# A hybrid attention / Fourier / product-key step on one core: two of five block rankings are moved in among the output projections

## The reference

```
h   = rmsnorm(x, norm1_g) * (1 + sc1) + sh1
q, k, v, f = split(h @ w_in)
x  += g1 * (concat(headnorm(diff_attention(q, k, v)), fourier_mix(f)) @ w_out)     # "merge"
h2  = rmsnorm(x, norm2_g) * (1 + sc2) + sh2
q   = (h2 @ w_query)                      # 8 heads x 2 halves x 128
s   = q . sub_keys                        # 128 scores for each head and half
s1, i1 = top16(s[:, :, 0]);  s2, i2 = top16(s[:, :, 1])
top_s, pos = top16(s1[i] + s2[j])         # 16 of the 16 x 16 pairs
idx = i1 * 128 + i2 (at pos);  g = softmax(top_s)
a   = gelu(expert_u[idx] . h2);   x += g2 * sum(g * a * expert_v[idx])
y   = rmsnorm(x, final_g)
```

## Time and profile before

| | us |
|---|---|
| time, median of 3 runs | 1900.49 (1897.9 to 1902.98) |
| time of the profiled execution | 1900.14 |
| its span | 1898.2 |
| busy in the span: TensorE, VectorE, ScalarE, GpSimd | 1740.1, 1522.8, 681.9, 794.9 |
| merge starts on TensorE | 360.28 |
| first ranking done, dense gates start | 503.91 |
| last dense gates stored, issued | 745.43 |
| first dense sum | 806.77 |

### The profile page before, as it was taken

The page is one execution under the profiler, slowest core; times in us unless marked ns, Lnnn a source line. Parts: engine busy times, 40 slices in busy tenths (PEclk is TensorE's granted clock), DMA queues, the critical chain, the costliest instruction groups (busy, mean ns, idle before and its releaser), DMA issues.

```text
span 1898.2 us, 29868 instructions
## 1 busy us (share of the span) xinstructions
PE 1740.1 (92%) x9942; PEld 1490.9 (79%) x9942; DVE 1522.8 (80%) x3093; ACT 681.9 (36%) x1135; POOL 794.9 (42%) x646
## 2 busy tenths in 40 slices
PE   4789998897899999389999999999999999999994
PEld 2477746547788888279999999999999999999993
DVE  0342127334999999879999999999999999999997
ACT  1132226301367674223333333333333333333332
POOL 1300000000000000267887887778666666666661
PEclk9989989899999999689999999999999999999997
DMA  9921200520044445699999999999999999999993
GB/s 358 386 80 50 89 0 1 214 85 23 1 90 90 90 109 130 226 353 408 405 402 392 405 400 405 407 403 403 394 407 407 407 402 398 403 399 407 405 403 138
DMA packets 253538, 520.89 MB, mean 274 GB/s; under 512 B 113953, under 2 KB 130977, under 8 KB 252193
## 3 DMA queue, kind: packets, MB, share of 16 engines
q1 hardware_dynamic: 178016, 249.00, 36.9%
q0 software_dynamic: 73728, 268.47, 35.7%
q10 hardware_dynamic: 1730, 2.59, 0.4%
HBM read 488.54 MB, written 31.46 MB: 274 GB/s over the span
## 4 chain that ended last, share of the span: by engine, by line
PE 52%; DVE 25%; issue 13%; DMA 6%; ACT 3%; DVEq 1%; SPq 0%; POOL 0%; ACTq 0%; POOLq 0%
DVE arena L1155 12%; PE ps L1522 9%; PE ps L1521 9%; PE ps L1520 9%; PE ps L1440 5%; PE ps L1421 4%; DMA arena_w<-in_w_mod 4%; PE ps L1491 3%; DMA U_in<-in_expert_uT 2%; PE ps L1275 2%; PE ps L1279 2%; PE ps L1276 2%; PE ps L1319 1%; DVE V_lo L1117 1%; DVE C_lo L1130 1%
## 5 line engine op out<-in xcount | busy, mean ns | idle before, releaser
L1520 PE MATMUL ps<-hT_hi,U_hi 128*128 128x384 f32 x1024 | 344.4, 336 | 29.5 <-DVE U_lo L1112 29.5
L1522 PE MATMUL ps<-hT_hi,U_lo 128*128 128x384 f32 x1024 | 344.5, 336 | 0.0
L1521 PE MATMUL ps<-hT_lo,U_hi 128*128 128x384 f32 x1024 | 343.7, 336 | 0.0
L1520 PE MATMUL ps<-V_hi,C_hi 128*128 128x512 f32 x768 | 300.4, 391 | 11.0 <-DVE C_lo L1130 11.0
L1522 PE MATMUL ps<-V_hi,C_lo 128*128 128x512 f32 x768 | 302.3, 394 | 0.0
L1521 PE MATMUL ps<-V_lo,C_hi 128*128 128x512 f32 x768 | 302.3, 394 | 0.0
L1520 PEld LDWEIGHTS ps<-hT_hi,U_hi 128*128 128x128 f32 x1024 | 193.0, 188 | 34.6 <-issue 29.7
L732 ACT CAST V_hi<-V_in 128x1024 fp32r<-128x1024 f32 x128 | 135.1, 1055 | 235.9 <-PE ps L1522 235.9
L458 POOL DMA_INDIRECT arena<-in_expert_u,idxn x128 | 171.5, 1340 | 99.1 <-DVE arena L1144 37.8
L740 ACT ACTIVATE act_t<-ps 128x384 f32<-128x384 f32 x128 | 63.0, 492 | 410.0 <-PE ps L1522 410.0
L458 POOL DMA_INDIRECT arena<-in_expert_v,idxn x128 | 159.5, 1246 | 93.1 <-DVE arena L1155 41.1
(11 more groups left out here) (230 smaller groups left out, 3233.2 us busy)
## 6 DMA issues: line engine op xcount, KB each, us to landing
U_in<-in_expert_uT SPq DMA_DIRECT2D x128, 512.0 KB, 9.1
V_in<-in_expert_v SPq DMA_DIRECT2D x128, 512.0 KB, 6.4
arena_w<-in_w_mod SPq DMA_DIRECT2D x12, 2048.0 KB, 12.4
gates_scratch<-arena_w SPq DMA_DIRECT2D x6, 4096.0 KB, 20.8
gate_in<-gates_scratch SPq DMA_DIRECT2D x128, 192.0 KB, 7.4
arena_w<-in_w_in SPq DMA_DIRECT2D x4, 2048.0 KB, 12.4
arena_w<-in_w_query SPq DMA_DIRECT2D x1, 7168.0 KB, 20.6
arena_w<-in_w_out SPq DMA_DIRECT2D x2, 2048.0 KB, 7.8
```

The source lines that it names most:

```text
L1520: nc.tensor.matmul(out, hi, rhi, start=start, stop=False)
L1521: nc.tensor.matmul(out, hi, rlo, start=False, stop=False)
L1522: return nc.tensor.matmul(out, lo, rhi, start=False, stop=stop)
```

## The change

The order of the rankings becomes 0, 1, 2, 3, 4. Rankings of block 0 and 1 stand among the merges: TensorE's list is now written out by hand, halves of merges between query groups, with turns of h2 where a block's h2 is first needed. Dense gates of blocks 1, 2, 3 stand beside the rankings of 2, 3, 4, and no ranking stands alone behind them. The fetched blocks stay 0 and 4, in the other order.

To allow that: merges use PSUM banks 4 to 7; x is loaded into H2 itself, so h2 of a block overwrites x1 in place and waits until x1 of that block is stored (`s_spill[b]`); squares are taken by halves. In the last ranking all 32 quads stand in the first three groups; hT_lo and two U_lo stand between the third and the fourth. The sum over one-hot rows (`tensor_reduce`) becomes four additions. SyncE's list issues U of groups 2 and 3, all of XF and fing ahead of H2s, V and gates.

```diff
-SPARSE = (4, 0)
+SPARSE = (0, 4)
-ORDER = (1, 2, 3, 4, 0)
-FIN = (4, 0, 1, 2, 3)
+ORDER = (0, 1, 2, 3, 4)
+FIN = (0, 4, 1, 2, 3)
+def dense_at(n):
+    return n - 1 if 2 <= n <= NDEN + 1 else 0
@@ sync
-            sp.wait_ge(s_wT, len(UNITS))
+            sp.wait_ge(s_chunk_used, DFT_C + 1)
             for b in range(NBLK):
-                sp.dma_start(X[:, b], xall[b * P:(b + 1) * P, :]).then_inc(s_xr[b], 16)
+                sp.dma_start(H2[b], xall[b * P:(b + 1) * P, :]).then_inc(s_xr[b], 16)
...
-                sp.dma_start(x1_d[b * P:(b + 1) * P, :], X[:, b]).then_inc(s_spill, 16)
+                sp.dma_start(x1_d[b * P:(b + 1) * P, :], H2[b]).then_inc(s_spill[b], 16)
...
             for b in range(1, NDEN + 1):
+                if b == NDEN:
+                    sp.wait_ge(s_fill2, B2.total)
+                    for j in range(2):
+                        load_u(j, j)
@@ vector: make_h2
+                link(dve.tensor_tensor(ss[:, b:b + 1], ss2[:, 0, b:b + 1], ss2[:, 1, b:b + 1], ALU.add))
                 dve.wait_ge(s_rstd2, b + 1)
-                link(dve.scalar_tensor_tensor(out=H2[b], in0=X[:, b], scalar=rstd[:, b:b + 1],
+                dve.wait_ge(s_spill[b], 16)
+                link(dve.scalar_tensor_tensor(out=H2[b], in0=H2[b], scalar=rstd[:, b:b + 1],
@@ vector: select
-                    link(dve.tensor_reduce(sel[:, w, :], onehot, AX.X, ALU.add))
+                    for n_ in (8, 4, 2):
+                        link(dve.tensor_tensor(onehot[:, :, 0:n_], onehot[:, :, 0:n_], onehot[:, :, n_:2 * n_], ALU.add))
+                    link(dve.tensor_tensor(sel[:, w, :], onehot[:, :, 0], onehot[:, :, 1], ALU.add))
@@ vector: the new order
+            merged(0, 0)
+            merged(0, 1)
+            make_h2(0)
...
+            merged(1, 0)
+            merged(1, 1)
+            make_h2(1)
+            ranked(0, 0)
+            merged(2, 0)
+            ranked(0, 1)
+            merged(2, 1)
+            ranked(0, 2)
+            make_h2(2)
+            merged(3, 0)
+            ranked(0, 3)
+            merged(3, 1)
+            dve.wait_ge(s_step, steps[0])
+            select(0)
+            make_h2(3)
+            gate_weights(0)
+            ranked(1, 0)
+            merged(4, 0)
+            ranked(1, 1)
+            merged(4, 1)
+            ranked(1, 2)
+            make_h2(4)
+            ranked(1, 3)
@@ vector: the last ranking
+                    for g in range(3):
+                        key_tops(n, g, bd, (2, 3, 2) if g else (0, 2, 2))
+                        dve.wait_ge(s_step, steps[0])
+                        pair_tops(g, bd, (1, 2, 1) if g else (2, 2, 2))
+                    dve.wait_ge(s_hThi, 1)
...
+                    split_u(0, 0)
+                    ranked(n, 3)
+                    split_u(1, 1)
+                    dve.wait_ge(s_step, steps[0])
+                    select(n, 0)
@@ tensor: the new order
+            merge(0, 0)
+            merge(0, 1)
+            merge(1, 0)
+            turn(0)
+            merge(1, 1)
...
+            turned(0)
+            part(0, 0)
+            score(0, 0)
+            merge(2, 0)
+            part(0, 1)
+            merge(2, 1)
+            score(0, 1)
+            turn(1)
+            part(0, 2)
+            merge(3, 0)
+            score(0, 2)
+            part(0, 3)
+            merge(3, 1)
+            score(0, 3)
+            turned(1)
+            part(1, 0)
+            merge(4, 0)
+            score(1, 0)
+            part(1, 1)
+            merge(4, 1)
+            score(1, 1)
+            part(1, 2)
+            score(1, 2)
+            turn(2)
+            part(1, 3)
+            score(1, 3)
+            turn(3)
+            turn(4)
+            turned(2)
+            part(2, 0)
+            score(2, 0)
+            part(2, 1)
+            score(2, 1)
+            pe.wait_ge(s_gated, 2 * NBLK)
```

More of the change, by code:

```diff
@@ L210, in program @@
         H2s = cutout(XO + 2 * D, D)
[L211 removed]
+        h2row = (H2[0], H2s)
         XF = cutout(MO, 5120).rearrange("p (b d) -> p b d", b=NBLK)
@@ L382, in _ @@
                 load_u(n, n % 2)
+            for b in range(NBLK):
+                sp.dma_start(XF[:, b], x1_d[b * P:(b + 1) * P, :]).then_inc(s_xf, 16)
+            sp.dma_start(fing, final_g.unsqueeze(0).broadcast_to([P, D])).then_inc(s_fing, 16)
+            sp.wait_ge(s_acc0, 1)
+            sp.wait_ge(s_h2out, 16)
+            sp.dma_start(H2s, h2_d).then_inc(s_h2in, 16)
+            for n in range(2, 4):
                 sp.wait_ge(s_vlo, n - 1)
                 load_v(n, n % 2)
[L385 to L391, removed]
+            sp.wait_ge(s_c, 1)
+            load_gates(2, 0)
             with sp.Fori(2, PAIRS) as i:
@@ L693, in sel_out, with softmax_exp @@
                     one_hot((b - 1) * QUADS + p)
[L695 to L702, removed]
+            def softmax_exp(n):
+                act.wait_ge(s_top, n + 1)
+                act.activation(top[:, :, :], top[:, :, :], ACT.Exp).then_inc(s_gexp, 1)
+            squares2(0)
+            turned(0)
+            squares2(1)
+            query_out(0, 0)
+            query_out(0, 1)
+            turned(1)
+            squares2(2)
+            query_out(0, 2)
+            query_out(0, 3)
+            squares2(3)
+            query_out(1, 0)
+            softmax_exp(0)
+            query_out(1, 1)
+            query_out(1, 2)
+            squares2(4)
+            turned(2)
+            query_out(1, 3)
+            turned(3)
+            turned(4)
+            query_out(2, 0)
+            query_out(2, 1)
+            softmax_exp(1)
+            for n in range(2, NBLK):
+                bd = dense_at(n)
+                sel_out(bd)
+                ahead = [(n, 2), (n, 3)] + ([(n + 1, 0), (n + 1, 1)] if n + 1 < NBLK else [])
                 for p in range(QUADS):
@@ L1097, in _ @@
             dve.memset(onesb[0:1, :], 1.0)
[L1098 to L1106, removed]
+            merged(1, 0)
[22 more added lines that the diff above has]
+            dve.wait_ge(s_step, steps[0])
+            select(1)
+            gate_weights(1)
             def split_u(n, r):
@@ L1416, in _, with merge, turn @@
             chunk_ready(OUT_C + 1)
[L1417 to L1421, removed]
-                                                start=(k == 0), stop=(k == KD - 1))
-                    last.then_inc(s_fill2, 1)
-            for b in range(NBLK):
+            def merge(b, half):
+                i = 2 * b + half
+                out = ps[:, 4 + i % 4, :]
+                if i >= 4:
+                    pe.wait_ge(s_gated, i - 3)
+                for k in range(KD):
+                    last = nc.tensor.matmul(out, mixT[:, k, b * P:(b + 1) * P], chunk[:, (OUT_C + half) % WRING, k, :],
+                                            start=(k == 0), stop=(k == KD - 1))
+                last.then_inc(s_merge, 1)
+            def turn(b):
                 pe.wait_ge(s_h2, b + 1)
@@ L1495, in dense_gates, with turned, part @@
                     differences(b, p + LR - 1)
+            def turned(b):
+                pe.wait_ge(s_act2, B2.emptied(B2.pos[("h2T", b, 1)])[1])
+            def part(b, g):
+                for j in range(4):
+                    query(b, g, j)
+            merge(0, 0)
[3 more added lines that the diff above has]
+            merge(1, 1)
             pe.wait_ge(s_wq, 16)
```

127 lines of the change are left out of this document (69 added, 58 removed).

## The result

The changed kernel takes 1908.36 us (median of 5 runs, 1905.19 to 1909.59) where the kernel before takes 1897.9 beside it (5 runs, 1897.44 to 1902.98): a ratio of 1.0046, 95% interval 1.0035 to 1.0057. It is slower, by 9 us when taken by the ratio and by 10.5 when taken by the medians. The forecast was 1909.5; rival A is what happened.

A forecast was written before the change was run, and what follows sets the result against it. TensorE was taken to bound the kernel. First dense sum at 825.1 instead of 806.8, less 8.9 regained by gelu of group 5, gave +9.4 on 1900.14: 1909.5 us, own range 1905 to 1914, overall range 1894 to 1917.

The forecast's parts named there:

- rival A: Whole kernel: the forecast itself, 1909.5 us, own range 1905 to 1914; chance 0.42.
- What bounds the kernel: Dense stages: TensorE with its queries sets the time, 80.4 us a stage, with VectorE close behind.
- The start: +37: Up to the first dense gates: TensorE's work, waits of 7.5 and 8, restarts of 4; gates at 540.9, 37 later.
- The additions: Rankings on VectorE: additions take 1.5 against 2.29 for the reduce, 1.6 off each ranking; full stages stay 80.4.
- The last stage: 70.9: Third dense stage: two query groups, then ScalarE sets the pace at 1.65 a quad; 70.9 against 80.4 before.
- H2s lands 27.2 behind the store: Queues behind the last store: 10.3 MB at about 410 GB/s, 25.2, plus 2 of latency; H2s lands at 820.8.
- What comes back: 8.9: First dense sum to gelu of group 5: U of group 4 no longer late, 34.9 instead of 43.8, 8.9 regained.
- The sum: +9.4: Whole kernel: first dense sum at 825.1 less 806.8, less 8.9 regained, gives +9.4 on 1900.14.
- B: Behind the last store: H2s or later loads come earlier by other queue sharing or overtaking, 1897 to 1903; chance 0.24.
- C: At the start: TensorE runs without its two waits and restarts, 19.5 earlier, 1890; one wait, 1900; chance 0.13 for faster.
- D: Start or last stage: VectorE is late at more scores or falls behind, 5 to 10 more, 1915 to 1920; chance 0.16.
- E: Dense stages: they hang on VectorE and the additions pay, 3 to 5 less than forecast, 1905; chance 0.05.

The follow-up runs named there:

- e9: The changed kernel with the four additions over one-hot rows put back to a tensor_reduce: 1909.26 us, ratio 1.0051 to the kernel before.
- e3: The changed kernel with the turn of block 0 behind the fourth merge half instead of the third: 1900.72 us, ratio 1.0011.
- e5: e3 with the turn of block 4 behind a query group of block 2, and score (2,1) moved into the dense stage: 1898.1 us, ratio 0.9996.
- e4: The changed kernel with the copy hT_hi of the last stage made by VectorE instead of ScalarE: 1906.57 us, ratio 1.0044.
- e1: The changed kernel with VectorE waiting for H2s only at its first use, in the second quarter of the fetched rows: 1900.78 us, ratio 1.0009.
- e6: The kernel before with only the changed kernel's SyncE list behind the last store of gates: 1897.54 us, ratio 0.9991.
- e7: e1 with the five XF and fing loaded one at a time, nine pairs apart, in the expert loop: 1893.48 us, ratio 0.9974.
- e8: The changed kernel with the edits of e5 and e7 in one: 1885.95 us, ratio 0.9934 to the kernel before.
- e2: e1 with XF and fing loaded in one piece four pairs before the expert loop's end: 1903.97 us, ratio 1.0022.

## Why the prediction was right, step by step

- **What bounds the kernel.** TensorE does; held, with a small rest. The two full stages took 699.00 - 540.04 = 159.0, that is 79.5 each, against a forecast of 80.4 from the earlier trace rows. The step said that the additions don't touch them; by e9's trace they take 0.8 off the two together. The other 1.0 is not accounted for.
- **The start: +37.** `gate_weights` of block 1 came 180.7 after the merge's start, forecast 180.6. The wait of block 0 was 7.53 (forecast 7.5), that of block 4 7.7 (8), two restarts about 2 each. One step was right in size and not quite in its cause: at block 4 the turn waited first 3.58 for h2 and then 4.08 for the bank, where I had put it all on the bank. Both come from VectorE's list being behind. e3 shows by removal that the first wait is worth 7.6 and doesn't move elsewhere; e5 shows that the second does, to `gate_weights`.
- **The additions: mis-sized.** I took 1.5 for them against 2.29 for a reduce. They took 2.06 from their start to the next operation, so they save 0.26 and not 0.8 each:

```profile
785.18 1.60 DVE L1092 TENSOR_TENSOR arena<-arena 128x1024 bf16<-128x1024 bf16 x3
786.82 0.39 DVE L1093 TENSOR_TENSOR sel<-arena 128x128 f32<-128x128 bf16 x1
787.24 2.29 DVE L1085 TENSOR_TENSOR arena<-arena,places 128x2048 bf16<-128x2048 bf16 x1
```

  The Trainium skill ("VectorE: DVE Perf Modes", Rules for kernel authors) advises to restructure a tensor_reduce. Here that took away a tenth of it.
- **The last stage: 70.9.** It took 768.88 - 699.00 = 69.9. ScalarE's pace is 1.63 a quad and hT_hi 2.74, as forecast; e4 shows by removal that hT_hi is on the path (24.25 against 26.15 for the stretch). **The store: 21.0.** It took 20.9.
- **H2s lands 27.2 behind the store.** It was 29.4. The bytes were 10.84 MB (forecast 10.3) and the mean rate 369 GB/s, not 410. The rate was low at the beginning, when GpSimd's fetches on q0 hadn't begun:

```profile
789.80:795.00 5.20, 0.00 (x0) 0.00 (x0) 4.85 (x11) 1.90 (x2) 3.53 (x4) 0.51 0.72 221
795.00:800.00 5.00, 0.00 (x0) 0.00 (x0) 2.71 (x3) 1.91 (x4) 4.09 (x4) 0.50 1.01 399
```

  H2s itself was issued late, at 797.55, as it waited until VectorE had cleared its sums (L1277); by then the queues were full, and no run shows whether that cost anything. The 2 us of latency in the forecast's sum is shown by no row of its own either. This 2.2 was the largest error, and the earlier steps together had an opposite one of 2.8: that the sum came within 0.3 of the 9.15 at group 5 is partly luck. From H2s to the first sum 4.1 (forecast 4.3).
- **What comes back: 8.9.** Gelu of group 5 came 35.5 after the first sum (forecast 34.9, before 43.8): 8.3 regained.
- **The sum: +9.4.** In the profiled executions it is 9.6 of span: 9.15 at group 5, 1.4 more behind the last gelu, less 1.0 by which the front was earlier. From group 5 to the last gelu both kernels take 1013.4; behind it the change takes 35.6 and the kernel before 34.2, and e1, e3, e4, e5, e6 and e9, which keep that part as it is, take 34.2 to 34.6. Neither the 1.4 nor the 1.0 was in any step.
- **The rivals.** B (H2s earlier) didn't happen: the queue kept its order. C (no waits at the start) didn't happen: both waits were there. Its price for one wait held (1900; e3 1900.7), that for both (1890) did not: e5 takes both away and stays at 1898.1, because VectorE's `gate_weights` then make TensorE wait 7.95. D's late VectorE shows only as the 3.58. E is right in kind at most for the 0.8 of e9, not for 3 to 5.

One idea of the working proved too simple: that the change loses because the ranking that hid the store is gone. The store is bare, but e7 and e8 keep it bare and are faster than before. What is lost hangs as well on what stands in the queue behind it, and on where its data is waited for.

## What to carry to other kernels

When cover is taken away from a stretch of transfers, read the queue behind it in order of issue and ask of each entry who waits for it first; entries wanted only at the end (here 3.1 MB of XF and fing) belong behind those, and in a loop whose transfers are near their bound they go in singly, not in a row. And a wait should stand at the first use of its data, not at the first call of a helper that may use it. When a stall is removed, look for the next owner: here VectorE's `gate_weights`, then the loop's own transfers and VectorE's last rows.

## What was unexpected of the hardware

- A loop that moves 408 GB/s with TensorE always busy took six extra loads of 0.5 MB at a cost of 0.5 up to the last gelu when they came singly, from 938.58 to 1688.56 (e7), and lost 14 us when they came within 3 us (e2: 11.04 of waiting, and a restart at the lower clock). The mean rate doesn't tell the two apart.
- The Trainium skill ("DMA: Bandwidth & Descriptors", Specifications) gives about 358 GB/s as the limit of device memory for one core, worked out as half of what two cores share. In the first two windows of e2 above one core, the only one that the program uses, moved 408 and 397; the measurement decides.
- One transfer of 0.5 MB takes anything from 3.3 us (V, the first behind the store) to 21.7: H2s 21.7, U of group 4 16.4 and 21.1. These three were issued behind XF and fing on their own queue, with the fetches busy on the other.
